# The last but one expert tile is stored like the others, in a two-layer backbone with routed experts

## The chip, the core and the metric

The kernel runs on one core of a Trainium2 chip. The metric is device time in microseconds (us) of one execution, the median of the runs shown.

## The reference

A backbone block of two layers works on 1024 latent tokens of width 1024 (layer 0 also on 256 context tokens). Layer 0 mixes the tokens with gated linear attention and a long convolution, layer 1 with a short gated convolution. Each layer ends in a mixture of experts: a token picks one group of four, and in it two experts of eight (32 experts in all, hidden width 512):

```python
def run_block(args):
    tok, e = args
    xb = x_pad[tok]
    return (jax.nn.silu(xb @ w1[e]) * (xb @ w3[e])) @ w2[e]
...
y = yb.reshape(P, D) * slot_g[:, None]
return jax.ops.segment_sum(y, slot_t, num_segments=T + 1)[:T]
...
h = h + m_lat[5] * f.reshape(B, S, D)
return rmsnorm(h, norm_final)
```

So each token gets the sum of two expert rows, each times its gate, added to the stream h. All is float32. Every expert's three matrices are 2 MB each, 6 MB per expert and 201 MB per layer.

## The kernel before

**Tiles.** Each expert has room for 96 assignments (CAP). The 32 x 96 places are cut into NP = 24 tiles ("passes") of 128 rows, 0 to 23; a tile spans two experts. Tile 22 uses experts 29 and 30, tile 23 experts 30 and 31. Tokens beyond an expert's 96 go to an overflow branch, which is skipped when there are none; all engines still read its flag and add to semaphores (`ov_left`) that the next stage waits for.

**A pass.** GpSimd gathers the tile's token rows from memory (L822). VectorE turns them into columns (`x_cols`). TensorE makes the up products, two for each tile (`pass_ups`, L1709, 64 instructions each, 128 in all), ScalarE takes silu of the first (L1189), VectorE multiplies (`pass_hidden`, L2497), TensorE transposes the hidden rows (`turn_hidden`, L1686), ScalarE copies them to the arena as HT (L1191), and TensorE makes the down product (`pass_down`, L1744). VectorE multiplies it with the layer's output gate into YS, two buffers by parity of the tile (`pass_rows`, L2542), and GpSimd stores YS to the DRAM tensor `expert_rows` by an indirect DMA, each row at its token's place (`scatter`, L835). On TensorE the down product of tile p-1 stands between the up products and the transposes of tile p.

**Weights.** SyncE loads the weights (`moe_weights`, L562), in halves of 1 MB, into slots by the parity of the expert. A half of expert e+2 is asked for when the products on the same half of expert e are over (`half_mm`, `up_mm`, `gate_mm`, `y_mm`). Expert 30's down weights are asked for by the down product of tile 21, half of them at its middle and half at its end; expert 31's by that of tile 22.

**Late tiles.** With NL = NP // 2 - 1 = 11, tiles 0 to 21 are stored. Tiles 22 and 23 are late: they stay in YS, and their rows are brought to the tokens by matrix products. For that, in passes 3 to 11, VectorE makes gated one-hot matrices for one block of 128 tokens a pass (`gated_hot`), for each late tile and each of a token's two choices; TensorE transposes and adds the choices (`late_hot`, L1720, 8 instructions a block), and VectorE copies them to LATE_HOT. There is a gate table for stored rows (GM[:, 0]), one for overflow rows and one for each late tile.

**Rows back.** When tile 21's store is done, SyncE loads the rows of each block of 128 tokens (`rows_back`, L542, 1 MB, eight per layer) into three buffers CY; from the fourth on a load waits until VectorE has used its buffer. VectorE adds them, gated, to H (`add_rows`, L2482 and L2484). In its order, block 0 comes behind tile 21's gating, blocks 1 to 3 between pass_hidden(23) and pass_rows(22), blocks 4 to 7 behind that, and pass_rows(23) last. On SyncE some of these loads stand ahead of expert 31's down weights. CY[2] lies over the columns XT of both parities.

**Sums.** Then, when all engines have passed the overflow branch, TensorE multiplies LATE_HOT with YS (`late_sums`, L1821), per block two halves of 512 columns and two late tiles, each product two instructions: 64 per layer. VectorE adds them to H (`add_late`, L2628). In layer 0 the RMS norm of layer 1 follows block by block: ScalarE's squares and roots, VectorE's scaling, TensorE's transposes (L1835), ScalarE's columns (L1111), then the projections of the short convolution: plain products (L1843) of the first half of the tokens, of the second half, and then Strassen products (L1869). In layer 1 the final norm follows (L2669) and SyncE stores the output (L723).

**Spares.** `spare(n, b)` issues n products into an unused bank (L1240). Twelve stand between the transposes of tile 23 and its down product.

Of the kernel before, what the change touches and what calls it, by code (L numbers as in the profile page):

```python
# [108 lines left out]
def build(nc, a, out):  # L109
    with ExitStack() as ctx:  # L110
# [50 lines left out]
        NL = NP // 2 - 1  # L161
# [108 lines left out]
        CY = [at(base, 2, D) for base in (34720, 24576, 26624)]  # L270
        CY_LOADS = [len(range(b, TT, NCY)) for b in range(NCY)]
        GM = at(37700, 4, 2, TT)
        HOT_GATED = at(34720, 2, 2, P)
        LATE_HOT = [at(47104, SEQ), at(33056, SEQ)]
# [238 lines left out]
        def _(sp):  # L513
# [32 lines left out]
            def moe_weights(l):  # L546
# [33 lines left out]
                for p in range(NP):  # L580
# [10 lines left out]
                    if p == NP - 1:  # L591
                        for b in range(2):
                            sp.wait_ge(y_out[b], 16 * NL * (l + 1))
                        for i in range(2):
                            rows_back(2 * l, i)
                        sp.wait_ge(gate_mm, n0 + NP)
                        for i in range(2, 4):
                            rows_back(2 * l, i)
                    if freed_down:
                        sp.wait_ge(half_mm, halves_before(l, p) + 3)  # L600
                        for e in freed_down:
                            weights(e, 2, (0,))
                        if p == NP - 1:
                            rows_back(2 * l, 4)
# [3 lines left out]
                for i in range(5, TT):  # L608
                    rows_back(2 * l, i)
# [118 lines left out]
        def _(pool):  # L728
# [98 lines left out]
            def scatter(l, p):  # L827
# [3 lines left out]
                if l or p >= 2:  # L831
                    pool.wait_ge(y_out[b], (l * NL + p // 2) * 16)
# [6 lines left out]
            def experts(l):  # L839
# [11 lines left out]
                for p in range(NP):  # L851
# [5 lines left out]
                    if p < 2 * NL:  # L857
                        scatter(l, p)
                for b in range(2):
                    pool.wait_ge(y_out[b], NL * (l + 1) * 16)  # L860

# [371 lines left out]
        def _(pe):  # L1233
# [462 lines left out]
            def experts(l):  # L1696
# [63 lines left out]
                for p in range(NP):  # L1760
# [6 lines left out]
                spare(12, 0)  # L1767
# [43 lines left out]
            def late_sums(l, i):  # L1811
# [100 lines left out]
        def _(dve):  # L1912
# [362 lines left out]
            def mix_and_route(l, tmp):  # L2275
# [150 lines left out]
                place_, late = SC[:, 8:10], float(2 * NL)  # L2426
# [358 lines left out]
```

## Time and profile before

| what | value |
|---|---|
| median of the three timed runs | 2500.44 us (2494.41 to 2502.44) |
| profiled execution, first to last instruction (the page gives this span, and no other time of it) | 2494.6 us |
| TensorE busy with matmuls | 2372.1 us, 95% |
| VectorE, ScalarE, GpSimd busy | 1143.0, 361.5, 294.1 us |
| DMA, HBM read | 550.74 MB |
| weights of the experts (L562) | 384 loads of 1 MB, median 10.5 us to landing |
| rows back (L542) | 16 loads of 1 MB, median 7.7 us to landing |
| stores of tiles (L835) | 44 |

The shares are averages over stages. The expert stages lie from about 860 to 1413 us (layer 0) and from about 1903 to 2459 us (layer 1); the page's DMA line shows them as the stretches with 380 to 410 GB/s. PE is TensorE's matmul, PEld its weight load, DVE VectorE, ACT ScalarE, POOL GpSimd, SP SyncE. A float32 matmul is two instructions, so counts are twice what the code shows.

### The profile page before, as it was taken

To read this page: it belongs to the slowest core of one execution; us is meant where nothing else is said; L and a number is where in the kernel's file an instruction comes from. 1 tells how busy PE (TensorE), PEld (TensorE's weight loads), DVE (VectorE), ACT (ScalarE), POOL (GpSimd) and SP (SyncE) were. 2 spreads that over 40 slices of the span, in tenths; PEclk is the share of its full clock that TensorE was granted. 3 is DMA by queue.
4 is the path that set the end of the run, shared out by engine and by line. 5 is a ranking of instruction groups with operands and counts; after the bars stand their busy time and mean duration, and the time that the engine had idled before them with its cause. 6 is when DMAs were issued, how large, how long until landed. Compare 5 with 4: busy or idle time off the path is not lost. (4 is left out here: it accounts for less than half of the span.)

```text
span 2494.6 us, 33367 instructions
## 1 busy us (share of the span) xinstructions
PE 2372.1 (95%) x14149; PEld 1058.1 (42%) x14150; DVE 1143.0 (46%) x2405; ACT 361.5 (14%) x645; POOL 294.1 (12%) x313
## 2 busy tenths in 40 slices
PE   4999999989999999999999899999999999999997
PEld 3545444544555523333233344444555333334433
DVE  1788377767945423322222544434455223322226
ACT  2310233331012200000000240000121000000002
POOL 2000000001000222122220000000002122221200
PEclk9999999999999999999999999999999999999999
DMA  9577100020170599999999611112106999999994
GB/s 307 200 251 275 34 26 26 17 110 34 68 286 34 213 357 402 402 404 413 388 409 410 240 34 51 34 51 85 76 29 254 378 406 402 414 402 414 406 379 202
DMA packets 140530, 581.41 MB, mean 233 GB/s; under 512 B 16756, under 2 KB 41640, under 8 KB 87768
## 3 DMA queue, kind: packets, MB, share of 16 engines
q1 hardware_dynamic: 120648, 534.87, 55.1%
q0 software_dynamic: 19648, 44.09, 4.8%
q8 instruction: 114, 1.87, 0.3%
q10 hardware_dynamic: 80, 0.26, 0.0%
q14 instruction: 40, 0.33, 0.0%
HBM read 550.74 MB, written 44.32 MB: 239 GB/s over the span
## 5 line engine op out<-in xcount | busy, mean ns | idle before, releaser
L1709 PE MATMUL ps<-arena 128*32 128x512 f32 x6144 | 678.9, 595 | 16.8 <-DMA arena<-in_ex_w_dram 16.8
L1709 PEld LDWEIGHTS ps<-arena 128*32 128x32 f32 x6144 | 207.2, 110 | 440.7 <-issue 423.7
L1744 PE MATMUL ps<-arena 128*32 128x512 f32 x3072 | 344.2, 598 | 11.2 <-DMA arena<-in_ex_w_dram 11.1
L1869 PE MATMUL ps<-arena 128*128 128x512 f32 x616 | 264.5, 592 | 0.0
L2497 DVE TENSOR_TENSOR arena<-arena,ps 128x512 f32<-128x512 f32 x48 | 52.3, 1090 | 456.2 <-PE ps L1709 456.2
L1589 PE MATMUL ps<-arena 128*128 128x512 f32 x512 | 229.4, 598 | 1.6 <-DVE arena L2273 1.6
L1744 PEld LDWEIGHTS ps<-arena 128*32 128x32 f32 x3072 | 119.1, 111 | 226.2 <-issue 207.5
L822 POOL DMA_INDIRECT arena<-normed_rows,arena x184 | 185.7, 1009 | 111.6 <-issue 52.5
L2542 DVE TENSOR_TENSOR arena<-ps,gates 128x512 f32<-128x512 f32 x96 | 61.8, 686 | 257.4 <-PE ps L1744 257.4
L1869 PEld LDWEIGHTS ps<-arena 128*128 128x128 f32 x616 | 117.0, 190 | 147.3 <-issue 147.3
L1402 PE MATMUL ps<-arena 128*128 128x512 f32 x384 | 167.3, 593 | 0.7 <-issue 0.7
L1589 PEld LDWEIGHTS ps<-arena 128*128 128x128 f32 x512 | 94.3, 190 | 105.3 <-issue 103.3
L835 POOL DMA_INDIRECT expert_rows<-arena x44 | 45.1, 1025 | 700.4 <-DVE arena L2542 660.1
L1191 ACT ACTIVATE arena<-ps 128x512 f32<-128x512 f32 x48 | 28.7, 597 | 650.4 <-PE ps L1686 650.4
L1402 PEld LDWEIGHTS ps<-arena 128*128 128x128 f32 x384 | 72.0, 190 | 88.1 <-issue 87.6
L2523 DVE TENSOR_SCALAR arena<-arena,gain_x,mod 128x128 f32<-128x128 f32 x368 | 98.6, 370 | 1.7
L2022 DVE SCALAR_TENSOR_TENSOR arena<-arena,silu_c 128x512 f32<-128x512 f32 x120 | 90.2, 752 | 4.3
L842 POOL DMA_DIRECT2D normed_rows<-arena x16 | 8.6, 538 | 667.2 <-ACT arena L1157 667.2
L1189 ACT ACTIVATE arena<-ps 128x512 f32<-128x512 f32 x48 | 28.7, 597 | 352.2 <-PE ps L1709 204.7
L1320 PE MATMUL ps<-arena 128*128 128x512 f32 x160 | 74.1, 616 | 2.5 <-ACT arena L935 2.5
L2681 DVE TENSOR_TENSOR arena<-arena 128x512 f32<-128x512 f32 x11 | 7.6, 693 | 140.2 <-PE ps L1869 140.2
L2515 DVE STREAM_TRANSPOSE arena<-arena 128x256 f32<-128x256 f32 x184 | 65.2, 412 | 9.6 <-DMA arena<-normed_rows,arena 7.0
(325 smaller groups left out, 2297.0 us busy)
## 6 DMA issues: line engine op xcount, KB each, us to landing
arena<-in_ex_w_dram SPq DMA_DIRECT2D x384, 1024.0 KB, 10.5
arena<-in_mod_w_dram SPq DMA_DIRECT2D x24, 2048.0 KB, 8.7
arena<-expert_rows SPq DMA_DIRECT2D x16, 1024.0 KB, 7.7
arena<-in_od_w_in_dram SPq DMA_DIRECT2D x12, 1024.0 KB, 5.4
arena<-in_x_dram SPq DMA_DIRECT2D x2, 4096.0 KB, 15.4
expert_rows<-gates SPq DMA_DIRECT2D x8, 1024.0 KB, 22.4
normed_rows<-arena POOLq DMA_DIRECT2D x16, 512.0 KB, 2.9
arena<-in_ev_w_in_dram SPq DMA_DIRECT2D x3, 2048.0 KB, 13.1
```

The source lines that it names most:

```text
L822: pool.indirect_dma_start(XG[:, b, t * 256:(t + 1) * 256], None, row_pieces, bass.IndirectOffsetOnAxis(ap=PIECE[:, t * NP + p:t * NP + p + ...
L1320: ins = nc.tensor.matmul(bank((2, 3, 6)[i % 3]), u_cols(i, j), w[:, j], start=j == 0, stop=j == KC - 1)
L1402: ins = nc.tensor.matmul(bank(6 + half), HYP[n % 3][:, j], u_part(half, j), start=j == 0, stop=j == KC - 1)
L1589: ins = nc.tensor.matmul(bank(m % 4), mixed[:, j, i * P:(i + 1) * P], weights[half][:, j], start=j == 0, stop=j == KC - 1)
L1709: ins = nc.tensor.matmul(bank(2 + m)[c:c + n], x[:, j, c:c + n], w_slot(e % 2, m, KC, FE)[:, j], start=j == 0, stop=j == KC - 1)
L1744: ins = nc.tensor.matmul(bank(5 + half)[c:c + n], HT[:, j * P + c:j * P + c + n], w_slot(e % 2, 2, FC, D)[:, j, half * 512:(half + 1) * 51 ...
L1869: ins = nc.tensor.matmul(bank(4 * (g % 2) + b), x[:, j], y[:, j], start=first and j == 0, stop=j == 3, skip_group_check=True)
L2022: link(V.scalar_tensor_tensor(out=acc, in0=w[:, j], scalar=silu_c[:, j, 0:1], in1=acc, op0=ALU.mult, op1=ALU.add))
L2497: return V.tensor_tensor(HS.rearrange("t (c p) -> t p c", p=P), SL.rearrange("t (p c) -> t p c", c=FC), bank(3).rearrange("t (p c) -> t p ...
L2515: ins = V.transpose(XT[:, b].rearrange("p (j t) -> p j t", j=KC)[:, :, 32 * t:32 * t + 32], XG[:, b, t * 256:(t + 1) * 256].rearrange("p ( ...
L2523: ins = V.tensor_scalar(x, x, gain_x[:, 2 * l + 1, j:j + 1], mod[:, l, 3, j:j + 1], ALU.mult, ALU.add)
L2542: V.tensor_tensor(YS[:, b, cs], bank(5 + half), gates[:, 1, cs], ALU.mult).then_inc(y_ready, 1)
```

## The change

Tiles 0 to 22 are stored, only tile 23 is late.

- TensorE: the loop over tiles ends at 22; then three spares, the down product of 22, the up products of 23, six spares, the transposes of 23, three spares, the down product of 23.
- One late tile instead of two: half of the one-hots (VectorE), of their transposes (TensorE), of their copies, and of the sums (L1821). VectorE's copy of a one-hot signals by itself.
- VectorE's order at the end: pass_rows(22), pass_hidden(23), blocks 0 to 3, pass_rows(23), blocks 4 to 7.
- SyncE: no row is loaded before both parities' stores are done, tile 22's with them; expert 31's down weights come before all row loads.
- The second half of CY[2] moves off the odd XT buffer.
- The waits for stores count by parity (12 even and 11 odd tiles per layer).

```diff
-        NL = NP // 2 - 1
+        STORED = [len(range(b, NP - 1, 2)) for b in range(2)]
...
-        CY = [at(base, 2, D) for base in (34720, 24576, 26624)]
+        CY = [at(34720, 2, D), at(24576, 2, D), at(26624, 2, 6432)[:, :, 0:D]]
...
-        HOT_GATED = at(34720, 2, 2, P)
-        LATE_HOT = [at(47104, SEQ), at(33056, SEQ)]
+        HOT_GATED = at(34720, 2, P)
+        LATE_HOT = at(47104, SEQ)
...
@@ SyncE, moe_weights @@
-                    if p == NP - 1:
-                        for b in range(2):
-                            sp.wait_ge(y_out[b], 16 * NL * (l + 1))
-                        for i in range(2):
-                            rows_back(2 * l, i)
-                        sp.wait_ge(gate_mm, n0 + NP)
-                        for i in range(2, 4):
-                            rows_back(2 * l, i)
                     if freed_down:
-                        sp.wait_ge(half_mm, halves_before(l, p) + 3)
+                        sp.wait_ge(half_mm, halves_before(l, p) + 3 if p < NP - 1 else 3 * NP * l + 3 * (NP - 1))
                         for e in freed_down:
                             weights(e, 2, (0,))
-                        if p == NP - 1:
-                            rows_back(2 * l, 4)
                         sp.wait_ge(y_mm, n0 + p)
                         for e in freed_down:
                             weights(e, 2, (1,))
-                for i in range(5, TT):
+                for b in range(2):
+                    sp.wait_ge(y_out[b], 16 * STORED[b] * (l + 1))
+                for i in range(TT):
                     rows_back(2 * l, i)
...
@@ GpSimd @@
-                    if p < 2 * NL:
+                    if p < NP - 1:
                         scatter(l, p)
...
@@ TensorE, late_hot and the end of experts @@
-                    for q in range(2):
-                        for k in range(2):
-                            ins = nc.tensor.matmul(bank(7)[:, q * P:(q + 1) * P], HOT_GATED[:, q, k], ident,
-                                                   start=k == 0, stop=k == 1)
+                    for k in range(2):
+                        ins = nc.tensor.matmul(bank(7)[:, 0:P], HOT_GATED[:, k], ident, start=k == 0, stop=k == 1)
...
-                for p in range(NP):
+                for p in range(NP - 1):
                     pass_ups(p)
                     if p:
                         pass_down(p - 1)
                     else:
                         pe.wait_ge(tab_ready, l + 1)
                     turn_hidden(p)
-                spare(12, 0)
+                spare(3, 0)
+                pass_down(NP - 2)
+                pass_ups(NP - 1)
+                spare(6, 0)
+                turn_hidden(NP - 1)
+                spare(3, 0)
                 pass_down(NP - 1)
...
@@ TensorE, late_sums @@
-                    for q in range(2):
-                        ins = nc.tensor.matmul(bank(SUM_BANKS[i % 2][half]), LATE_HOT[q][:, i * P:(i + 1) * P],
-                                               YS[:, q, half * 512:(half + 1) * 512], start=q == 0, stop=q == 1)
+                    ins = nc.tensor.matmul(bank(SUM_BANKS[i % 2][half]), LATE_HOT[:, i * P:(i + 1) * P],
+                                           YS[:, (NP - 1) % 2, half * 512:(half + 1) * 512], start=True, stop=True)
...
@@ VectorE, experts @@
                 for p in range(NP):
                     if p + 1 < NP:
                         x_cols(p + 1)
+                    if p == NP - 1:
+                        pass_rows(p - 1)
                     pass_hidden(p)
-                    if p == NP - 1:
-                        for i in range(1, 4):
-                            add_rows(2 * l, i, GM[:, 0])
-                    if p:
+                    if p and p < NP - 1:
                         pass_rows(p - 1)
                     if 4 <= p < 4 + TT:
                         late_hot(p - 4)
                     if 3 <= p < 3 + TT:
                         gated_hot(p - 3)
-                    if p == NP - 2:
-                        add_rows(2 * l, 0, GM[:, 0])
+                for i in range(4):
+                    add_rows(2 * l, i, GM[:, 0])
+                pass_rows(NP - 1)
                 for i in range(4, TT):
                     add_rows(2 * l, i, GM[:, 0])
-                pass_rows(NP - 1)
```

The waits for stores in `scatter`, `pass_rows`, `experts` and `overflow_tables` read `STORED[b]` in place of `NL`, the gate tables have one entry less, and `gated_hot` and VectorE's `late_hot` loop over one tile.

## Rows read from the trace of the kernel before

**Rows 1.** Chain of waits: start us, us, what.
```profile
2418.40 6.14 DMA expert_rows<-arena
...
2424.61 4.84 DMA arena<-expert_rows
...
2458.70 27.75 PE ps L1821 x64
```

**Rows 2.** Stretches: length, busy time per engine, granted clock, DMA share, GB/s.
```profile
940.00:1112.00 172.00, 171.00 (x1548) 56.80 (x1544) 58.47 (x165) 9.55 (x16) 40.57 (x40) 1.00 1.00 401
...
2160.00:2430.00 270.00, 262.56 (x2396) 98.68 (x2388) 67.89 (x171) 14.34 (x24) 48.61 (x48) 1.00 0.99 403
```

**Rows 3.** Timeline, TensorE, layer 0: start us, us, engine, line, operation.
```profile
1100.41 0.66 PE L1686 MATMUL ps<-constants,arena 128*128 128x128 f32 x4
...
1122.96 0.66 PE L1686 MATMUL ps<-constants,arena 128*128 128x128 f32 x4
...
1144.29 0.66 PE L1686 MATMUL ps<-constants,arena 128*128 128x128 f32 x4
```

**Rows 4.** Timeline, TensorE, end of layer 1.
```profile
2416.13 0.66 PE L1686 MATMUL ps<-constants,arena 128*128 128x128 f32 x4
...
2416.72 13.94 PE L1709 MATMUL ps<-arena 128*32 128x512 f32 x128
...
2430.48 7.05 PE L1744 MATMUL ps<-arena 128*32 128x512 f32 x64
...
2437.46 0.66 PE L1686 MATMUL ps<-constants,arena 128*128 128x128 f32 x4
...
2437.95 5.34 PE L1240 MATMUL ps<-constants 128*128 128x256 f32 x24
...
2447.09 8.66 PE L1744 MATMUL ps<-arena 128*32 128x512 f32 x64 [3.79 <-DMA arena<-in_ex_w_dram]
```

**Rows 5.** Timeline, TensorE, end of layer 0.
```profile
1369.22 0.66 PE L1686 MATMUL ps<-constants,arena 128*128 128x128 f32 x4
...
1401.13 9.39 PE L1744 MATMUL ps<-arena 128*32 128x512 f32 x64 [4.75 <-DMA arena<-in_ex_w_dram]
...
1413.06 7.33 PE L1821 MATMUL ps<-arena 128*128 128x512 f32 x13 [2.53 <-DVEq L2619]
...
1476.58 43.94 PE L1869 MATMUL ps<-arena 128*128 128x512 f32 x102
```

**Rows 6.** DMA, 2423 to 2424, then 1375 to 1376: packets, MB, share.
```profile
q1 hardware_dynamic: 3, 0.01, 2.0%
...
q1 hardware_dynamic: 5, 0.02, 4.0%
```

**Rows 7.** Stretch 1401 to 1405, as rows 2.
```profile
1401.00:1405.00 4.00, 3.87 (x20) 1.12 (x24) 1.60 (x3) 0.00 (x0) 0.00 (x0) 0.50 1.01 426
```

**Rows 8.** Timeline, VectorE, end of layer 1.
```profile
2409.23 1.09 DVE L2497 TENSOR_TENSOR arena<-arena,ps 128x512 f32<-128x512 f32 x1 [9.67 <-PE ps L1709]
...
2449.35 1.28 DVE L2482 SCALAR_TENSOR_TENSOR arena<-arena 128x1024 f32<-128x1024 f32 x1 [2.35 <-DMA arena<-expert_rows]
...
2451.87 1.28 DVE L2482 SCALAR_TENSOR_TENSOR arena<-arena 128x1024 f32<-128x1024 f32 x1
...
2456.91 1.28 DVE L2542 TENSOR_TENSOR arena<-ps,gates 128x512 f32<-128x512 f32 x2
```

**Rows 9.** Timeline, VectorE, finish of layer 1.
```profile
2467.45 1.28 DVE L2669 SCALAR_TENSOR_TENSOR arena<-arena,rstd,gates 128x1024 f32<-128x1024 f32 x1
...
2469.30 0.69 DVE L2628 TENSOR_TENSOR arena<-ps,arena 128x512 f32<-128x512 f32 x1 [0.57 <-PE ps L1821]
```

**Rows 10.** Timeline, ScalarE, behind the sums of layer 0.
```profile
1427.71 2.88 ACT L1111 ACTIVATE arena<-ps,mod,gain_x 128x128 f32<-128x128 f32 x8
...
1430.96 1.06 ACT L1099 ACTIVATE arena<-arena 128x1024 f32<-128x1024 f32 x1 [0.28 <-DVE arena L2628]
...
1432.02 2.88 ACT L1111 ACTIVATE arena<-ps,mod,gain_x 128x128 f32<-128x128 f32 x8
```

More of the change, by code:

```diff
@@ L831, in scatter @@
                 if l or p >= 2:
-                    pool.wait_ge(y_out[b], (l * NL + p // 2) * 16)
+                    pool.wait_ge(y_out[b], (l * STORED[b] + p // 2) * 16)
                 if l == 0 and p == 0:
@@ L856, in experts @@
                         pool.dma_start(GF, a["norm_final"].partition_broadcast(P)).then_inc(small_in, 16)
-                    if p < 2 * NL:
+                    if p < NP - 1:
                         scatter(l, p)
                 for b in range(2):
-                    pool.wait_ge(y_out[b], NL * (l + 1) * 16)
+                    pool.wait_ge(y_out[b], STORED[b] * (l + 1) * 16)
             def overflow(l):
@@ L2425, in mix_and_route @@
                 link(V.tensor_tensor(GATE[:, 1], GATE[:, 0], SC[:, 4], ALU.mult))
-                place_, late = SC[:, 8:10], float(2 * NL)
+                place_, late = SC[:, 8:10], float(NP - 1)
                 step(V.scalar_tensor_tensor(out=GM[:, 1], in0=place_, scalar=float(CAP), in1=GATE,
@@ L2430, in mix_and_route @@
                                             op0=ALU.is_lt, op1=ALU.mult))
-                for q in range(2):
-                    step(V.scalar_tensor_tensor(out=GM[:, 2 + q], in0=PASS_OF, scalar=late + q, in1=GM[:, 0],
-                                                op0=ALU.is_equal, op1=ALU.mult))
+                step(V.scalar_tensor_tensor(out=GM[:, 2], in0=PASS_OF, scalar=late, in1=GM[:, 0],
+                                            op0=ALU.is_equal, op1=ALU.mult))
                 link(V.scalar_tensor_tensor(out=GM[:, 0], in0=PASS_OF, scalar=late, in1=GM[:, 0],
@@ L2449, in overflow_tables @@
                 for b in range(2):
-                    dve.wait_ge(y_out[b], 16 * NL * (l + 1))
+                    dve.wait_ge(y_out[b], 16 * STORED[b] * (l + 1))
                 place_, tile, slot = [SC[:, q:q + 2].rearrange("p k t -> p (k t)") for q in (8, 10, 12)]
@@ L2537, in pass_rows @@
                     if l or p >= 2:
-                        dve.wait_ge(y_out[b], (l * NL + p // 2) * 16)
+                        dve.wait_ge(y_out[b], (l * STORED[b] + p // 2) * 16)
                     for half in range(2):
@@ L2544, in gated_hot @@
                 def gated_hot(i):
-                    for q in range(2):
-                        for k in range(2):
-                            step(V.tensor_scalar(HOT_GATED[:, q, k], cst[:, K_IOTA:K_IOTA + P],
-                                                 SC[:, 12 + k, i:i + 1], GM[:, 2 + q, k, i:i + 1],
-                                                 ALU.is_equal, ALU.mult))
+                    for k in range(2):
+                        step(V.tensor_scalar(HOT_GATED[:, k], cst[:, K_IOTA:K_IOTA + P], SC[:, 12 + k, i:i + 1],
+                                             GM[:, 2, k, i:i + 1], ALU.is_equal, ALU.mult))
                     settle()
@@ L2556, in late_hot @@
                     dve.wait_ge(sum_mm, 2 * TT * l + i + 1)
-                    for q in range(2):
-                        step(V.tensor_copy(LATE_HOT[q][:, i * P:(i + 1) * P], bank(7)[:, q * P:(q + 1) * P]))
-                    settle()
-                    dve.sem_inc(late_ready, 1)
+                    V.tensor_copy(LATE_HOT[:, i * P:(i + 1) * P], bank(7)[:, 0:P]).then_inc(late_ready, 1)
                 first_x_cols()
```

2 lines of the change are left out of this document (1 added, 1 removed).

## The prediction

> **What bounds the kernel now.** Three views were read. First the chain of waits at the end: it goes through the store of tile 21's rows, the loads of the rows, the additions on VectorE and then 27.75 us of summing matmuls, 2458.70 to the last tile [rows 1]. So the last 76 us of the span hang on rows and sums, and layer 0's expert stage ends in the same way [rows 5]. Then the stretches: while tiles pass, the 16 DMA engines are busy 0.99 to 1.00 of the time at 401 to 403 GB/s, and TensorE nearly all of it too [rows 2]. Last the timeline around the change, of TensorE [rows 4, 5], VectorE [rows 8, 9] and ScalarE [rows 10].
>
> Below, D is the moment at which down(22), the down product of the last but one tile, is over, and T the moment at which the summing matmuls start. Before, D is 2437.46 and T 2458.70 in layer 1 [rows 4, 1]; T is 1413.06 in layer 0 [rows 5].
>
> **Step 1, down(22) comes forward, and its weights are late.** TensorE ends down(21) at 2416.13 and the transposes at 2416.72 [rows 4]. Twelve spare products take 5.34 us [rows 4], so three take 1.33, and down(22) could start at 2418.05 (ScalarE's copy of the hidden columns lies beside the spares). It needs the second half of expert 30's down weights. SyncE asks for that half when down(21) is over, at 2416.15, behind what is still in the queue; before, another 14 us of up products lay between the request and the use. The weights' queue still moves packets in the stretch from 2423 to 2424, though nothing was asked of it after 2416.15; in layer 0 it does so from 1375 to 1376, after a request at 1369.25 [rows 6]. I take 2423.9 and 1376.1 as landings. So TensorE idles 5.9 us in layer 1 and (ready at 1369.22 + 0.59 + 1.33 = 1371.15 [rows 5]) 4.95 us in layer 0.
>
> After such an idle the granted clock is the lower of the two levels, 1.2 GHz: 0.50 from 1401 to 1405, after 4.75 us without work [rows 5, 7]. The down product there took 9.39 us, and 8.66 after 3.79 us of idle, against 7.05 [rows 4, 5]: 1.6 to 2.3 us, I take 2.2. TensorE: Matmul & The Clock Gate in the Trainium skill (HAM oscillation) says that a wait on a DMA between bursts of matmuls brings the gate back to half rate; by that rule this edit makes a new place of the kind, and the trace agrees at the two places just named.
>
> D is then 2423.95 + 6.98 + 2.2 = 2433.15 in layer 1 and 1376.15 + 9.2 = 1385.3 in layer 0. With no late weights it would be 2425.05 and 1378.1; these are the other ends.
>
> **Step 2, the rows wait for tile 22's store.** After D: gating on VectorE and issue by GpSimd 2.25 us (down(21) ended 2416.13, the store went out 2418.40), store 6.14, first load 4.84 [rows 1, 4]: the first rows are there at D + 13.3, the next two 2.6 us apart (1 MB at 403 GB/s). Beside it TensorE runs ups(23), 13.76 us (2416.72 to 2430.48), six spares 2.67, the transposes 0.59, three spares 1.33, down(23) 6.98 [rows 4]: D + 25.35. Its weights were asked for at D at the latest and are covered by ups(23); the 3.79 us that down(23) waited for them before [rows 4] go.
>
> VectorE, in its order: pass_hidden(23) holds the queue until the gate product is done, and takes 1.09 us [rows 8]: D + 14.95. So the store and the first load are hidden with 1.7 us to spare. Then four times 2.52 us for add_rows (2449.35 to 2451.87 [rows 8]): D + 25.05; the loads from the fourth on go out when a buffer is free and are back 4.84 later, 17.5 + 4.84 = 22.3 for the fourth, needed at 22.5. pass_rows(23) waits for TensorE and ends at D + 26.8 (1.28 [rows 8]); four more add_rows, D + 36.9. From the last add_rows to the first sum lay 1.7 us, 0.5 of it behind the end of the gating at 2458.19 [rows 8, 1]; without that gating in between I take 1.1. **T = D + 38.0**: 2471.15 and 1423.3, which is 12.45 and 10.25 later than before. Without the late weights it would be 4.35 and 3.05 later.
>
> Why so much, when D comes 4.3 us earlier? Before, all loads but three were out before D and the additions of four tiles ran beside tile 23; now all eight start behind the store of tile 22, and four of them are left when TensorE is done.
>
> DMA: Bandwidth & Descriptors in the Trainium skill (Queues, rings and completion order) says that an engine goes round its queues packet by packet, so that a store on GpSimd's queue doesn't stand behind all weights of SyncE's. By that rule the store would take little over its own 0.5 MB, some 3 us less than 6.14; T stays, because the store is hidden behind pass_hidden(23).
>
> **Step 3, half the summing.** The 64 instructions per layer become 32. Layer 1: TensorE gave a tile each 3.47 us (27.75 by eight [rows 1]) and VectorE waited 0.57 us of them [rows 9]. So VectorE bounds at 2.9 us: 6 intervals of 0.57, 3.4 us. The first tile: before, VectorE scaled it 8.75 us after T (2467.45 [rows 9]), held by TensorE; now ScalarE's square and table load behind the first addition hold it, and TensorE starts at the lower clock after 12 us of idle, for which I take 8.1. Gain 4.1 us (bounds 2.5 to 5.5). Layer 0: from T to the first Strassen product TensorE had 63.5 us of work in a row [rows 5]; 13.8 of it go (32 x 0.43), but ScalarE needs per tile 4.31 us of which only 0.28 were idle [rows 10], and the second half of the first projections needs all eight tiles. First columns at T + 15, eight tiles at 4.03, the last two without squares: T + 43.4; behind it 32 x 0.43 = 13.8 us: 57.2. Gain 6.3 us (bounds 1.5 to 13.8).
>
> **Step 4, half the transposed one-hots.** A pass with them takes 22.55 us, one without 21.33 [rows 3]. Half is 0.61 us, times 16 passes 9.8 us of TensorE. But the DMA engines are full in these passes and also in those after [rows 2], where TensorE waits for weights; time won in one is waited for in the next. I take 0.7 per layer, 1.4 in all (bounds 0 and 9.8). VectorE's saved copies and gates lie beside TensorE: nothing. The one store more, 0.5 MB, is in step 2. The spares are twelve as before: nothing.
>
> **Sum.** 12.45 + 10.25 - 4.1 - 6.3 - 1.4 = +10.9 us. On the profiled span of 2494.6 that is 2505.5. The page gives no other time of that execution; the three timed runs are 2494.4 to 2502.4, and the span is at their low end, so the same step stands on the median of 2500.4: **2511 us**.
>
> **Rivals.**
> - The DMA engines have room, and what TensorE saves in step 4 is kept: +10.9 + 1.4 - 9.8 = +2.5, 2503. For it: in the passes with one-hots TensorE never waits. Against: DMA share 1.00 there [rows 2].
> - The half of expert 30 is there when down(22) wants it (the late packets of rows 6 would be another transfer's): 8.1 and 7.2 us go, -4.4, 2496. Against: rows 6 in both layers. This alone would be no measurable change.
> - The other sign: the queue of weights has room, and TensorE, ahead by 0.61 us a pass, keeps this lead and asks earlier, so that expert 30's half meets an empty queue and lands within 1.9 us of the time it is needed. It decides at the request behind down(21): then -4.4 + 1.4 - 9.8 = -12.8, 2488. Against: a load lands 4.84 us after its issue even at a free queue [rows 1], and the lead has to survive eleven passes in which TensorE waits for weights now.
> - The store of tile 22 and the last weights hinder each other, and T comes 2 to 4 us later in each layer: 2515 to 2519. For it: 1.7 us is all the slack that the store has.
>
> **How the numbers follow.** A run of this kernel tells 0.3% (7.5 us) from no change. Chances: forecast 0.57 (its own range 2505 to 2516), rival one 0.17, two 0.11, three 0.05, four 0.10. Slower by over 0.3% (above 2508): four, and most of the forecast, 0.61. Within: rivals one and two and the low end of the forecast, 0.33. Faster: the third, 0.06. Range: 2497 to 2519; it leaves out the third rival, half of the second and a tail above.
>
> **What would show it.** A wait of TensorE for in_ex_w_dram ahead of down(22) in both layers, 5 to 6 us, and the lower clock after it; the first row load some 8 us after D and not before; no such wait ahead of down(23); the first sum 38 us after D; a VectorE without idle in layer 1's finish, 2.9 us a tile; first Strassen product some 57 us after T in layer 0; passes 4 to 11 at 21.9 us with new waits for weights in between. I am wrong if down(22) starts without a wait, or if the expert stage up to tile 21 ends 4 us or more earlier than now.

## Result

The median of nine runs is 2513.8 us (2504.7 to 2518.7), of the kernel before 2500.4 us (2494.4 to 2513.5). The ratio is 1.0056, 95% interval 1.0039 to 1.0073: **slower by 14 us** (10 to 18). Forecast was 2511, slower.

The profiled execution has a span of 2516.9 us, at the upper end of its runs, where the one before (2494.6) is at the lower end of its own; so the two profiles differ by 22.3 us, and the part that is not in the timed difference has to be told from the part that is. From the page after:

```profile
span 2516.9 us, 33051 instructions
...
PE 2345.2 (93%) x14021; PEld 1017.1 (40%) x14022; DVE 1127.7 (45%) x2355; ACT 360.8 (14%) x645; POOL 295.8 (12%) x315
```

TensorE's end of layer 1, which answers to [rows 4]; columns as there. L1678 are the transposes, L1232 the spares, L1734 the down products, L1701 the up products, L1815 the sums.

```profile
2428.27 0.66 PE L1678 MATMUL ps<-constants,arena 128*128 128x128 f32 x4
...
2437.05 9.98 PE L1734 MATMUL ps<-arena 128*32 128x512 f32 x64 [6.83 <-DMA arena<-in_ex_w_dram]
2446.84 13.92 PE L1701 MATMUL ps<-arena 128*32 128x512 f32 x128
...
2463.39 0.60 PE L1678 MATMUL ps<-constants,arena 128*128 128x128 f32 x4
...
2465.21 7.07 PE L1734 MATMUL ps<-arena 128*32 128x512 f32 x64
2485.49 5.43 PE L1815 MATMUL ps<-arena 128*128 128x512 f32 x6 [13.20 <-DVEq L2606]
```

The down product of tile 22 now follows the transposes, after 6.83 us of wait for weights, and takes 9.98 us instead of 7.05. The wait of 3.79 us ahead of the last down product [rows 4] is gone. The sums start 57.2 us after the transposes of tile 22 (2428.27 to 2485.49), 42.6 before [rows 4, 1]. Layer 0, for [rows 5]:

```profile
1370.66 0.66 PE L1678 MATMUL ps<-constants,arena 128*128 128x128 f32 x4
...
1378.75 8.37 PE L1734 MATMUL ps<-arena 128*32 128x512 f32 x64 [6.14 <-DMA arena<-in_ex_w_dram]
1386.93 13.92 PE L1701 MATMUL ps<-arena 128*32 128x512 f32 x128
...
1428.86 2.04 PE L1815 MATMUL ps<-arena 128*128 128x512 f32 x2 [16.49 <-DVEq L2606]
```

VectorE and SyncE at the end of layer 1, for [rows 8]: the first load goes out at 2454.21, VectorE comes to the first addition at 2461.79, held by pass_hidden(23), and adds without a gap for loads to 2483.8.

```profile
2454.21 22.36 SPq L542 DMA_DIRECT2D arena<-expert_rows  x8
...
2460.89 1.05 DVE L2490 TENSOR_TENSOR arena<-arena,ps 128x512 f32<-128x512 f32 x1 [12.44 <-PE ps L1701]
2461.79 1.25 DVE L2475 SCALAR_TENSOR_TENSOR arena<-arena 128x1024 f32<-128x1024 f32 x1
...
2472.42 1.29 DVE L2535 TENSOR_TENSOR arena<-ps,gates 128x512 f32<-128x512 f32 x2 [0.51 <-PE ps L1734]
...
2482.49 1.28 DVE L2477 SCALAR_TENSOR_TENSOR arena<-arena 128x1024 f32<-128x1024 f32 x1
```

The finish of layer 1, for [rows 9]: TensorE now waits for VectorE, which scales a block every 2.78 us.

```profile
2496.51 1.28 DVE L2656 SCALAR_TENSOR_TENSOR arena<-arena,rstd,gates 128x1024 f32<-128x1024 f32 x1
...
2499.28 1.28 DVE L2656 SCALAR_TENSOR_TENSOR arena<-arena,rstd,gates 128x1024 f32<-128x1024 f32 x1
...
2499.24 1.98 PE L1815 MATMUL ps<-arena 128*128 128x512 f32 x4 [0.80 <-DVE arena L2615]
```

The waits for weights while tiles 0 to 22 pass in layer 0: engine, tile and line, releaser, us in total, times, longest. After:

```profile
PE ps L1701 <- DMA arena<-in_ex_w_dram: 12.5, 5, 4.4
...
PE ps L1734 <- DMA arena<-in_ex_w_dram: 2.8, 3, 1.2
```

The same before:

```profile
PE ps L1709 <- DMA arena<-in_ex_w_dram: 7.7, 4, 3.9
...
PE ps L1744 <- DMA arena<-in_ex_w_dram: 2.1, 2, 1.1
```

**Both executions, cut at the same instructions** (us; p0 and p22 are the starts of the transposes of tiles 0 and 22, L1686 before and L1678 after; first sum L1821 and L1815; first Strassen product L1869 and L1863):

| stretch | before | after | difference | forecast |
|---|---|---|---|---|
| start to p0 of layer 0 | 875.6 | 873.5 | -2.1 | 0 |
| layer 0, p0 to p22 | 493.6 | 497.2 | +3.6 | -0.7 |
| layer 0, p22 to first sum | 43.8 | 58.2 | +14.4 | +10.25 |
| layer 0, first sum to Strassen | 63.5 | 58.0 | -5.5 | -6.3 |
| Strassen to p0 of layer 1 | 448.2 | 445.5 | -2.8 | 0 |
| layer 1, p0 to p22 | 491.3 | 496.0 | +4.6 | -0.7 |
| layer 1, p22 to first sum | 42.6 | 57.2 | +14.7 | +12.45 |
| layer 1, first sum to end | 35.9 | 31.4 | -4.5 | -4.1 |

### The profile page after: what moved, and what is told of

It is laid out like the page before. It is cut to its first block, busy times and chain, and to the rows that moved or that the text cites. A ratio compares the mean times of both kernels' runs of the same rounds, so it can differ in the third digit from the quotient of the medians.

```text
span 2516.9 us, 33051 instructions
## 1 busy us (share of the span) xinstructions
PE 2345.2 (93%) x14021; PEld 1017.1 (40%) x14022; DVE 1127.7 (45%) x2355; ACT 360.8 (14%) x645; POOL 295.8 (12%) x315
## 4 chain that ended last, share of the span: by engine, by line
PE 72%; DMA 13%; DVE 11%; issue 2%; ACT 1%; SPq 0%; DVEq 0%; POOLq 0%
PE ps L1701 21%; DMA arena<-in_ex_w_dram 11%; PE ps L1863 11%; PE ps L1734 10%; PE ps L1581 9%; PE ps L1312 3%; PE ps L1357 2%; DVE arena L2115 2%; PE ps L1373 2%; PE ps L1394 2%; PE ps L1496 1%; PE ps L1515 1%; PE ps L1837 1%; PE ps L1232 1%; DMA arena<-in_mod_w_dram 1%
## 5 line engine op out<-in xcount | busy, mean ns | idle before, releaser
L1701 PE MATMUL ps<-arena 128*32 128x512 f32 x6144 | 681.6, 598 | 24.7 <-DMA arena<-in_ex_w_dram 24.7
L1701 PEld LDWEIGHTS ps<-arena 128*32 128x32 f32 x6144 | 198.7, 111 | 461.1 <-issue 459.5
L1734 PE MATMUL ps<-arena 128*32 128x512 f32 x3072 | 343.1, 598 | 18.7 <-DMA arena<-in_ex_w_dram 18.5
L2490 DVE TENSOR_TENSOR arena<-arena,ps 128x512 f32<-128x512 f32 x48 | 52.2, 1088 | 499.2 <-PE ps L1701 499.2
L1863 PE MATMUL ps<-arena 128*128 128x512 f32 x616 | 264.5, 592 | 0.0
L1734 PEld LDWEIGHTS ps<-arena 128*32 128x32 f32 x3072 | 106.7, 111 | 247.1 <-issue 247.0
L1863 PEld LDWEIGHTS ps<-arena 128*128 128x128 f32 x616 | 117.0, 190 | 147.3 <-issue 147.3
## 6 DMA issues: line engine op xcount, KB each, us to landing
expert_rows<-gates SPq DMA_DIRECT2D x8, 1024.0 KB, 22.3
arena<-in_ev_w_in_dram SPq DMA_DIRECT2D x3, 2048.0 KB, 13.6
```

The source lines that it names most:

```text
L1701: ins = nc.tensor.matmul(bank(2 + m)[c:c + n], x[:, j, c:c + n], w_slot(e % 2, m, KC, FE)[:, j], start=j == 0, stop=j == KC - 1)
L1734: ins = nc.tensor.matmul(bank(5 + half)[c:c + n], HT[:, j * P + c:j * P + c + n], w_slot(e % 2, 2, FC, D)[:, j, half * 512:(half + 1) * 51 ...
L1863: ins = nc.tensor.matmul(bank(4 * (g % 2) + b), x[:, j], y[:, j], start=first and j == 0, stop=j == 3, skip_group_check=True)
L2490: return V.tensor_tensor(HS.rearrange("t (c p) -> t p c", p=P), SL.rearrange("t (p c) -> t p c", c=FC), bank(3).rearrange("t (p c) -> t p ...
```

## Experiments

Theory A: the late weights and the chain store, loads, additions price the move (steps 1 and 2), the halved sums give back part (step 3), the halved one-hots next to nothing (step 4). The rivals are those of the prediction and those written with each run. Ratios are to the kernel before on the same chip, with 95% intervals. The same cuts for all kernels (us):

| kernel | p0 to p22, layers 0 / 1 | p22 to first sum, 0 / 1 | first sum to Strassen | first sum to end |
|---|---|---|---|---|
| before | 493.6 / 491.3 | 43.8 / 42.6 | 63.5 | 35.9 |
| after | 497.2 / 496.0 | 58.2 / 57.2 | 58.0 | 31.4 |
| after, again | 494.7 / 494.9 | 59.2 / 54.6 | 57.2 | 31.5 |
| no late weights | 495.9 / 493.6 | 50.7 / 49.2 | 57.2 | 31.4 |
| old order | 502.5 / 496.6 | 65.6 / 57.4 | 57.2 | 31.4 |
| no store of tile 22 | 496.6 / 493.1 | 58.5 / 55.0 | 57.7 | 31.4 |
| before, half sums | 496.9 / 497.4 | 43.9 / 42.4 | 55.9 | 29.6 |
| before, half sums and one-hots | 497.9 / 496.9 | 42.9 / 42.2 | 56.0 | 29.6 |
| up product ahead of down(22) | 499.6 / 491.9 | 57.5 / 52.3 | 57.1 | 31.5 |
| the same with early sums | 499.2 / 501.4 | 57.1 / 38.2 | 57.3 | 41.5 |
| that with forty copies more | 492.6 / 495.5 | 53.8 / 39.2 | 57.2 | 39.4 |
| before, early sums | 497.0 / 496.3 | 51.0 / 42.3 | 64.2 | 37.5 |
| before, weights first | 493.6 / 494.6 | 44.6 / 45.1 | 63.9 | 37.6 |
| before, both | 493.7 / 492.3 | 48.0 / 41.6 | 63.9 | 38.8 |

Where the sums start early, only the two end columns together can be compared.

**No late weights.**

```diff
 def pass_down(p):
-    weights_in(p, 2)
+    if p == NP - 2:
+        pe.wait_ge(w_full[1][2], (l * NE + 30) // 2 * 32)
+    else:
+        weights_in(p, 2)
...
-    w_slot(e % 2, 2, FC, D)
+    w_slot(1 if p == NP - 2 else e % 2, 2, FC, D)
```

> The changed kernel, but the down product of tile 22 reads expert 29's down weights for all its rows, so it does not wait for expert 30's (tile 22's rows for expert 30 are computed with other weights). Theory A (the late weights price the move of down(22)): TensorE has no idle ahead of down(22) and no lower clock in it, it ends 7.5 us (layer 0) and 9.7 us (layer 1) earlier, and the first sums follow it with the same 38 to 41 us: some 15 us faster than the changed kernel, about the time of the kernel before (-2 us). Theory B (the DMA engines set the chain: they are busy with the same weights to the same moment, so store and row loads behind them cannot come earlier): at most 5 us faster than the changed kernel, still 8 us or more slower than before.

Measured: 2496.9 us, ratio 0.9980 (0.9965 to 0.9995), some 19 us faster than the changed kernel by the two ratios. TensorE's timeline in layer 1:

```profile
2417.27 0.66 PE L1678 MATMUL ps<-constants,arena 128*128 128x128 f32 x4
...
2419.15 7.07 PE L1737 MATMUL ps<-arena 128*32 128x512 f32 x64
2426.04 13.92 PE L1701 MATMUL ps<-arena 128*32 128x512 f32 x128
...
2466.43 3.78 PE L1818 MATMUL ps<-arena 128*128 128x512 f32 x4 [14.94 <-DVEq L2609]
```

The idle and the lower clock are gone: the down product ends 8.8 us after the transposes started, not 18.6, and the first sums come 7.5 us (layer 0) and 8.1 us (layer 1) earlier than in the changed kernel, 15.6 in all. (The 19 us compare two chips, with some 6 us of uncertainty.) Theory A, by size too: with this one wait away, the change would be no loss. Store and row loads did move with the end of down(22) (first load 6.8 us behind it), so the DMA engines did not hold them. In layer 1, though, VectorE then waited 1.6 us for two of the later loads, so 8.1 of the 9.8 us came back there.

**Old order.** TensorE's and VectorE's order of before, tile 22 stored:

```diff
-for p in range(NP - 1):
+for p in range(NP):
...
-spare(3, 0)
-pass_down(NP - 2)
-pass_ups(NP - 1)
-spare(6, 0)
-turn_hidden(NP - 1)
-spare(3, 0)
+spare(12, 0)
 pass_down(NP - 1)
... and on VectorE:
-if p == NP - 1:
-    pass_rows(p - 1)
 pass_hidden(p)
-if p and p < NP - 1:
+if p:
     pass_rows(p - 1)
```

> The changed kernel with the order of before on TensorE and VectorE: up products of 23, down product of 22, transposes, twelve spares, down product of 23. Tile 22 is stored all the same and all row loads come behind its store. No late weights here. Theory A (what costs is the chain store of tile 22, loads, eight additions, whichever order it hangs on): down(22) ends 21 us after the transposes of tile 22 instead of 16.5 to 18.6, the rows come 13.3 us after that, then 8 x 2.52 + 1.28 + 1.1 us on VectorE: first sum 57 us after those transposes, as in the changed kernel (57.2 and 58.2); total within 4 us of the changed kernel, 10 to 17 us slower than before. Theory B (the late weights and the lower clock are the cause of the loss): they are gone, so 13 to 17 us faster than the changed kernel, no slower than before.

Measured: 2519.7 us, ratio 1.0069 (1.0049 to 1.0090). Within 4 us of the changed kernel with overlapping intervals, as theory A has it, and without any late weights: the move of down(22) gained nothing over the old place and lost nothing. The profile bears the expected 57 us out in layer 1 (57.4) and not in layer 0 (65.6). There VectorE waited for its loads during the additions too, and the stretch behind them took 4.3 us instead of 1.1:

```profile
1413.60 1.29 DVE L2470 SCALAR_TENSOR_TENSOR arena<-arena 128x1024 f32<-128x1024 f32 x1 [11.78 <-DMA arena<-expert_rows]
...
1418.34 1.28 DVE L2470 SCALAR_TENSOR_TENSOR arena<-arena 128x1024 f32<-128x1024 f32 x1 [2.13 <-DMA arena<-expert_rows]
...
1437.69 1.28 DVE L2470 SCALAR_TENSOR_TENSOR arena<-arena 128x1024 f32<-128x1024 f32 x1 [1.73 <-DMA arena<-expert_rows]
```

That execution was also the longest of its seven (2534.6 us; the others 2514.3 to 2522.9). What costs against the kernel before, in both orders, is that all eight additions come behind the down product of tile 22. In the old order it is the store and the first load that hold them. In the new order the late weights keep it from winning the time back; what else holds the first addition there, the next two experiments show.

**No store of tile 22.**

```diff
-STORED = [len(range(b, NP - 1, 2)) for b in range(2)]
+STORED = [len(range(b, NP - 2, 2)) for b in range(2)]
...
-if p < NP - 1:
+if p < NP - 2:
     scatter(l, p)
```

> The changed kernel without the store of tile 22 (its rows are left out of the output): the row loads need only the stores up to tile 21 and go out right behind expert 31's last weights, at the end of down(22), D. A look at the trace. Theory A (VectorE's order sets the additions: pass_hidden(23) holds the queue until D + 15): rows are there some 5 us earlier, the first addition still starts at D + 15, the first sums still 38 to 42 us after D (less 1 us in layer 0, where the fourth block waited for its load). Theory B (the store of tile 22 is on the path): the first sums come 6 to 8 us earlier after D in each layer.

One execution, 2517.4 us: the first load of layer 0 goes out at 1391.29, 0.7 us after down(22), not 6.7; the first addition waits for pass_hidden(23) all the same, and the sums start 58.5 and 55.0 us after p22 (layer 1: down(22) ended 2 us earlier after p22 than in the changed kernel's profile). Theory A: in the new order it is not the store that sets the start of the additions. Rows of SyncE and VectorE:

```profile
1391.29 29.68 SPq L542 DMA_DIRECT2D arena<-expert_rows  x8
...
1404.67 1.05 DVE L2490 TENSOR_TENSOR arena<-arena,ps 128x512 f32<-128x512 f32 x1 [12.45 <-PE ps L1701]
1405.57 1.25 DVE L2475 SCALAR_TENSOR_TENSOR arena<-arena 128x1024 f32<-128x1024 f32 x1
```

**Before with half of the sums, with and without half of the one-hots.**

```diff
-for q in range(2):
-    ins = nc.tensor.matmul(bank(SUM_BANKS[i % 2][half]), LATE_HOT[q][:, i * P:(i + 1) * P],
-                           YS[:, q, half * 512:(half + 1) * 512], start=q == 0, stop=q == 1)
+ins = nc.tensor.matmul(bank(SUM_BANKS[i % 2][half]), LATE_HOT[1][:, i * P:(i + 1) * P],
+                       YS[:, 1, half * 512:(half + 1) * 512], start=True, stop=True)
... and in the second kernel, in gated_hot and both late_hot:
-for q in range(2):
+for q in (1,):
```

> The kernel before with the sums for tile 23 alone, one-hots and their transposes as they were (tile 22's rows are left out of the output). The sums alone: 9.5 to 10.5 us faster than before. Against the run with half of the one-hots too: theory A the same within 2 us, theory B 8 to 10 us slower than that.

> The kernel before, its order and stores untouched, with one-hots, their transposes, copies and the sums for tile 23 alone (tile 22's rows are left out of the output). It holds what the change takes away and none of its costs. Theory A (time saved in passes 3 to 11 is waited for later): the ends give 9.5 to 10.5 us (5.3 in layer 0, 4.5 in layer 1) and the expert stages 0 to 2: 10 to 12 us faster than before. Theory B (TensorE's time in these passes counts, 0.61 us x 16): 18 to 20 us faster than before.

Measured: half sums 2489.3 us, ratio 0.9944 (0.9923 to 0.9965); with half one-hots 2484.2 us, 0.9930 (0.9910 to 0.9950). The sums alone give 14 us, more than the 10 expected: by the cuts 7.6 in layer 0 and 6.3 in layer 1, against 5.5 and 4.5 in the changed kernel. The one-hots add 3.5 us, with intervals that overlap; 9.8 is not seen, nor excluded by these times alone. The traces say more. For weights in layer 0, with full and with half one-hots:

```profile
PE ps L1709 <- DMA arena<-in_ex_w_dram: 10.6, 5, 3.9
...
PE ps L1744 <- DMA arena<-in_ex_w_dram: 1.3, 1, 1.3
```

```profile
PE ps L1709 <- DMA arena<-in_ex_w_dram: 13.0, 6, 4.5
...
PE ps L1744 <- DMA arena<-in_ex_w_dram: 2.2, 2, 1.2
```

With full one-hots TensorE waits 9.8 us (before) and 11.9, with half 15.3 (after) and 15.2; in layer 1 it is 9.5 and 13.3 against 14.9 and 14.3. A pass in which nothing is waited for does get shorter, 22.10 us instead of 22.55, but the waits in others make up for it (from the transposes of tile 8 to those of tile 9 in layer 0, 23.99 us in the changed kernel and 22.55 in the kernel before), and p0 to p22 is no shorter in either layer. The time is waited for. The profiles of the two kernels with half sums differ by 5.6 us, 5.0 of it ahead of tile 0 in the two layers and none in these passes.

**The first up product of tile 23 ahead of down(22).**

```diff
-spare(3, 0)
-pass_down(NP - 2)
-pass_ups(NP - 1)
+pe.wait_ge(xt_ready, 2 * (n0 + NP))
+pass_up(NP - 1, 0).then_inc(up_mm, 1)
+pass_down(NP - 2)
+pass_up(NP - 1, 1).then_inc(gate_mm, 1)
 spare(6, 0)
```

(SyncE's count of halves for expert 31's weights goes up by one with it.)

> The changed kernel with the first up product of tile 23 ahead of down(22), in the place of the three spares: it covers the wait for expert 30's weights and leaves only one up product between D and pass_hidden(23). Theory A: wait ahead of down(22) 0.5 to 1.5 us instead of 6 to 7, no lower clock in it, D 1.4 us (layer 0) and 2.8 us (layer 1) earlier; pass_hidden(23) at D + 8, so the first addition starts when the rows are there, D + 13.3 instead of D + 15; first sums at D + 36 to 38. 6 to 10 us faster than the changed kernel, 4 to 8 slower than before. Theory B (the row loads are then late one by one, as they were with the old order, and take the gain back): at most 4 us faster than the changed kernel.

Measured: 2510.4 us, ratio 1.0037 (1.0022 to 1.0052), 4 us faster than the changed kernel on the same chip, with intervals that overlap. The edit did what it should: 0.36 us of wait ahead of down(22) in layer 0, full clock. But VectorE, free 7 us earlier, now waits for each of the first four loads of layer 0 (3.35, 1.17, 2.88, 1.02 us) and for three of layer 1. The lines of layer 0:

```profile
1376.82 7.07 PE L1734 MATMUL ps<-arena 128*32 128x512 f32 x64 [0.36 <-DMA arena<-in_ex_w_dram]
...
1395.29 1.28 DVE L2476 SCALAR_TENSOR_TENSOR arena<-arena 128x1024 f32<-128x1024 f32 x1 [3.35 <-DMA arena<-expert_rows]
...
1399.06 1.28 DVE L2476 SCALAR_TENSOR_TENSOR arena<-arena 128x1024 f32<-128x1024 f32 x1 [1.17 <-DMA arena<-expert_rows]
...
1404.55 1.28 DVE L2476 SCALAR_TENSOR_TENSOR arena<-arena 128x1024 f32<-128x1024 f32 x1 [2.88 <-DMA arena<-expert_rows]
```

Against the first profile of the changed kernel layer 0 keeps 0.7 us of it and layer 1 4.9, against the second (below) 1.6 and 2.3. Theory B, mostly: my price for the loads (the first 4.84 us after its issue, the others 2.6 apart) was that of a free moment; the third is 5.5 us behind the second here. Together with the kernel without the store this shows that two things hold the first addition in the changed kernel, pass_hidden(23) at D + 15 and the chain of store and load at D + 11.6 and 12.3; taking one of them away gains no more than the distance to the other.

**Early sums on top of it,** and the changed kernel again:

```diff
 if i == 0:
-    pe.wait_ge(ov_left, 5 * (l + 1))
     pe.wait_ge(y_ready, 2 * NP * (l + 1))
     pe.wait_ge(late_ready, 4 * TT * l + 2 * TT)
+if i == 2:
+    pe.wait_ge(ov_left, 5 * (l + 1))
```

(TensorE also gets a wait inside the overflow branch, which is skipped here.)

> The kernel of the run before plus: TensorE makes the sums of blocks 0 and 1 as soon as tile 23's rows are gated, ahead of the common wait behind the overflow branch, where it idled for 10 us. The first addition of a sum then starts 1 us after that wait instead of 3.9, and the lower clock at the restart costs VectorE nothing: 3 us in each layer, 6 us faster than the run before. Rival: ScalarE's squares and table load follow the first addition and hold the second block, so only 1 to 2 us per layer are kept.

> The changed kernel itself, on the same chip as the two above: 1.0045 to 1.0065 of before, and the same rows as in its first profile (6 to 7 us of wait ahead of down(22), 57 to 58 us from tile 22's transposes to the first sums). If these intervals of the trace repeat to 1 us while the expert stages up to tile 21 differ by several, the stages are where the runs of one kernel differ.

Measured: early sums 2503.1 us, ratio 1.0005 (0.9987 to 1.0024); the changed kernel 2511.2 us, 1.0053 (1.0032 to 1.0073). Early sums take 8 us off (the two sets of runs leave 2 to 12). In layer 1 the sums start at 2467.96, 14 us before VectorE adds the first, and the two end columns together are 4.0 us shorter. In layer 0 they do not: the short convolution begins with a wait for `ov_left` of its own, which I had overlooked, and TensorE idled 23.7 us ahead of them; there the columns are 0.3 us shorter. The expected 3 us a layer came in one layer; the rest of the 8 us is in no stretch of these profiles. The repeat of the changed kernel has the same waits, somewhat shorter (5.74 and 5.57 us ahead of down(22) for 6.14 and 6.83), and 59.2 us in layer 0; layer 1's 54.6 is 2.6 below the first profile, 1.3 of it less wait and 1.4 less time in down(22), by when the clock came back.

**The kernel before with early sums, with the weights first, with both.** The first as above, plus the gating of tile 23 ahead of blocks 6 and 7; the second:

```diff
-if p == NP - 1:
-    rows_back(2 * l, 4)
 sp.wait_ge(y_mm, n0 + p)
 for e in freed_down:
     weights(e, 2, (1,))
+if p == NP - 1:
+    rows_back(2 * l, 4)
```

> The kernel before (two late tiles, its loads and its order on TensorE) with the early sums alone: VectorE gates tile 23 ahead of blocks 6 and 7, and TensorE makes the sums of blocks 0 and 1 before the common wait behind the overflow branch. TensorE bounds the sums there (3.47 us a block), so work done ahead of the wait is gained: the last block's sum comes 3 to 4 us earlier in layer 1 and 4 to 5 in layer 0, where the first eight products ran at the lower clock. 6 to 9 us faster than before. Rival: the down product of tile 23 ends at 2455.8, so the gating is only 1 us earlier than now and the sums start where they did: 0 to 2 us.

> The kernel before with one swap on SyncE: the second half of expert 31's down weights is asked for ahead of block 4's rows. The weights then land 2.5 us earlier, TensorE waits 1.3 us instead of 3.8 and 4.8 and keeps the clock, down(23) ends 4 us earlier; but VectorE's additions end when they did, and the sums wait for them: 0 to 2 us faster than before.

> Both. Down(23) ends at about 2451.6 instead of 2455.8, tile 23 is gated by 2453.2, and both early sums are done at the common wait, at 2459.5: 8 to 11 us faster than before, and 2 us or more faster than the kernel with early sums alone. Rival: block 4's rows come later by as much as the weights come earlier, VectorE's additions end 2.5 us later in each layer, and the kernel is no faster than with early sums alone.

Measured: 2506.8 us, ratio 1.0027 (1.0016 to 1.0038); 2502.9 us, 1.0017 (1.0007 to 1.0027); 2500.0 us, 0.9998 (0.9989 to 1.0008). None of the three came out as expected; only that both edits together beat the early sums alone by 2 us or more did (7 us).

Early sums: VectorE waits 5.0 us (layer 0) and 4.0 us (layer 1) for down(23) with two blocks still to add, TensorE starts 1 us behind the gating in layer 1, and layer 0 keeps its second wait. The end of layer 0 gets 7.9 us longer, that of layer 1 1.3.

Weights first, TensorE in layer 1, and the kernel before:

```profile
2446.87 7.07 PE L1744 MATMUL ps<-arena 128*32 128x512 f32 x64 [1.56 <-DMA arena<-in_ex_w_dram]
2463.27 11.95 PE L1821 MATMUL ps<-arena 128*128 128x512 f32 x23 [9.33 <-DVEq L2619]
```

```profile
2458.70 11.85 PE L1821 MATMUL ps<-arena 128*128 128x512 f32 x27 [2.95 <-DVEq L2619]
```

Counted from the transposes of tile 22, down(23) is over 3.8 us earlier, by the wait and the clock that it saved. But the sums start 2.6 us later, because VectorE waited longer for rows (block 4 3.64 us instead of 2.35, block 7 2.29 instead of none): this is the rival written with the third kernel. TensorE so idles 9.33 us instead of 2.95, and the sums start at the lower clock, 0.50 where it was 1.00: the first addition came 5.6 us behind the first sum (2463.27 to 2468.90), 3.8 before. The columns of the granted clock are the last but two, first with weights first, then the kernel before in layers 1 and 0:

```profile
2463.27:2465.27 2.00, 2.00 (x3) 0.96 (x4) 0.00 (x0) 0.00 (x0) 0.00 (x0) 0.50 0.01 4
```

```profile
2458.70:2460.70 2.00, 2.00 (x5) 1.04 (x6) 0.00 (x0) 0.00 (x0) 0.00 (x0) 1.00 0.00 0
...
1413.06:1415.06 2.00, 2.00 (x3) 0.97 (x4) 0.00 (x0) 0.00 (x0) 0.00 (x0) 0.50 0.26 55
```

So finishing early made the next start slower in layer 1, and later rows delayed it besides. In layer 0 the kernel before starts its sums at 0.50 already, after 2.53 us of idle, and little more was lost there.

With both edits the two ends are 6 us longer than in the kernel before by the profiles (4.5 and 1.9), while the timed runs are level; where the difference is regained was not found.

**Forty copies more.** In pass 14 of layer 0, on the kernel with early sums:

```diff
+if p == 14 and l == 0:
+    for z in range(40):
+        step(V.tensor_copy(HOT_GATED[:, 0, z:z + 1], cst[:, K_ONE:K_ONE + 1]))
+    settle()
```

> The kernel with the early sums on the changed one, plus forty copies of one column on VectorE in pass 14 of layer 0 into a free place, 3 us in a pass where VectorE idles for most of the time. They move VectorE's later instructions on by some forty places in its program. Theory A: the 2.5 us between the branch behind the overflow flag and its other side in layer 0 (0.6 us in the kernel before, and in layer 1 of all kernels) hang on where the target lies in the fetched program: they fall to about 0.6, and the sums of layer 0 start 1.9 us earlier after the last addition. Theory B: it hangs on how long the engines were idle or on the order of work there, and the 2.5 us stay. Total within 0.2% of the kernel before either way; no faster than it beyond the interval.

The chain of waits of the changed kernel behind the last addition of layer 0 (start us, us, what), and then of the padded one:

```profile
1425.56 0.07 DVEq L2574
1425.63 2.45 issue
1428.08 0.02 DVEq L2599
```

```profile
1422.50 0.07 DVEq L2581
1422.57 0.50 issue
1423.08 0.02 DVEq L2606
```

Theory A: 2.5 us between the branch and its other side (L2599) become 0.5 (L2606); in the kernel with early sums, from which the padded one is made, they are 2.40. 2503.5 us, ratio 1.0008 (0.9994 to 1.0022): 2 us are not to be told in the total.

## Why the prediction was right, and where not

- **What bounds the ends** (chain of rows, then sums): right. In the changed kernel, without late weights, without the store and in the old order, TensorE waits 13 to 31 us for VectorE ahead of the first sum.
- **Step 1, late weights.** Forecast: 5.9 and 4.95 us of idle and 2.2 us by the clock; measured 6.83 and 6.14, and 2.9 and 1.3 (9.98 and 8.37 against 7.05). Taking the wait away returned 7.5 us in layer 0, where wait and clock had cost 7.5, and 8.1 of 9.8 in layer 1.
- **Step 2, T = D + 38.** Measured 38.7 in layer 1 (2446.84 to 2485.49) and 41.9 in layer 0. "From the last add_rows to the first sum I take 1.1" was mis-sized: 1.7 in layer 1, 4.4 in layer 0, where the branch took 2.5. Another 1.1 is the wait for the fourth block's load in layer 0, which I had put at 0.2 us in hand; 0.5 of it stands in place of the wait for down(23). That the store is hidden behind pass_hidden(23) held, as the kernel without the store shows. The Trainium skill's rule that an engine goes round its queues (DMA: Bandwidth & Descriptors, Queues, rings and completion order) is borne out in its sign and not in its size: from the issue of tile 22's store to that of the first load it took 4.3 and 5.0 us, 1 to 2 us less than 6.14, where I had put 3 us less. It changed nothing, for the reason given.
- **Step 3.** 5.5 and 4.5 us for a forecast of 6.3 and 4.1. The kernels before with half sums got 7.6 and 6.3: the gap of 2 us in each layer comes of what precedes the sums. In the changed kernel TensorE idled 13 to 16 us there and began at the lower clock (0.50), in theirs 3 to 4; the first addition follows the first sum by 3.9 us in both layers, in theirs by 2.6 and 2.1. That is 1.2 and 1.8 us of the gap.
- **Step 4.** Nothing (forecast 0.7 a layer); the waits rose by 1 to 5.5 us a layer and the stage is no shorter. The saving itself was put too high: a pass without waits takes 0.45 us less, not 0.61, so rival one would have had 7.2 us to keep and not 9.8.
- **Sum.** With the measured ends of both profiles of the changed kernel the change costs +19.0 and +16.6 us. Between the Strassen products and tile 0 of layer 1 there are -2.8 and -2.3 us that were in no forecast: this stretch takes 445.5 to 446.1 us in some kernels and 447.7 to 448.2 in others, and the one-hots don't sort them (447.7 to 448.2 in four kernels with full ones, but 446.1 with early sums; 445.5 to 446.0 in those with half, but 447.7 in the padded one). Why stays open. That leaves 14 to 16; measured 14. The expert stages, +8.2 us in the profiled pair and +4.7 in the second profile, are not told from scatter: p0 to p22 takes 491.3 to 497.4 us over the kernels with full one-hots and 491.9 to 502.5 over those with half. The median came out 3 us above the forecast, and part of this closeness is luck: the end of layer 0 cost 5 us more than forecast, that of layer 1 2 us more in one profile and 1 less in the other, step 4 gave 1.4 less, and the 2 to 3 us of the stretch that nobody had counted took some of it back.
- **Rivals.** One (DMA engines have room) and three fell by the waits, two (expert 30's half is there in time) by the trace, four was half of it: the first sums came 2 to 4 us later than forecast, but by the terms named under step 2 and the longer wait of step 1, and not because the store hindered the weights: without the store the wait for the weights is there and the first sums come no earlier after D.

No kernel here that does all of the work beats the one before: the early sums on the changed kernel and both edits on the kernel before end level with it. Early sums in both layers, with layer 0's second wait moved as well, were not tried.

## What to carry to other kernels

A product moved forward needs its operands forward too: look up when its weights are asked for and what stands in the queue ahead of them, before counting what the move frees. Count a chain of store, load and additions from its new start, and see which instruction in the consumer's own queue lets it begin; here all eight additions slid behind one more down product, its store and the next tile's up products, for the sake of half the sums. And time saved on an engine that runs level with the DMA engines comes back as waits.

## What the runs showed of the hardware

- A TensorE that finishes early can start its next work at the lower of its two clock levels, 1.2 GHz: after 9.33 us of idle the sums began at 0.50 and VectorE's first addition came 5.6 us later; after 2.95 us they began at 1.00 and it came 3.8 us later. The length of the idle alone does not tell it: in layer 0 of the kernel before, the sums began at 0.50 after only 2.53 us, behind a down product that had itself begun at the lower clock after 4.75 us of idle. TensorE: Matmul & The Clock Gate (HAM oscillation) in the Trainium skill warns of gaps between matmuls; the trace agrees for the long gap, and adds that a gap behind work that ended sooner is one as well.
- The same branch on VectorE took 0.5 or 2.4 us to its other side: 2.4 in layer 0 in each of the six kernels made from the changed one without padding (seven profiles), 0.5 with forty instructions more ahead of it, and 0.5 in the kernels made from the one before. In all seven profiles with 2.4 us one packet of the queue q14 (kind: instruction) falls into the stretch, some 0.5 us behind the branch; in the profiles with 0.5 us none does. That fits a fetch of the program that VectorE waits for, but this was not tried by itself.
- Of three 1 MB row loads issued together on a free queue, the first landed after some 5 us. The longest of the eight loads of a layer took 12.1 to 13.6 us in layer 0 of the kernels made from the changed one, where four small broadcast loads of GpSimd's queue run beside them or just before, and 8.5 to 12.1 in layer 1, where none do. That the small loads are the cause was not tried, and the 12.1 us without them speak against their being the only one.
